# A two-layer model's kernel on one core: the opening of the first block re-ordered, adaLN dots placed anew, row remainders moved from GpSimd to VectorE

## What is computed

```
mod = silu(c) @ ada_w + ada_b                      # 6 x 1024 values; shift1, scale1, gate1, shift2, scale2, gate2
h   = rms_norm(x, norm1_g) * (1 + scale1) + shift1
z   = h @ w_in                                     # 1024 -> 3328: q, k, v of attention, seven parts for RWKV
att = dilated_mixture_attention(norm(q), norm(k), v)   # 8 heads, with a table of biases
rw  = rwkv7_bidirectional(token_shift(z[rest]))
x   = x + gate1 * (concat(att, rw) @ w_out)        # first residual projection
h2  = rms_norm(x, norm2_g) * (1 + scale2) + shift2
x   = x + gate2 * peer_ffn(h2)                     # top-16 experts of 16384, gathered rows
# second block: mod2 = silu(c_2) @ w_ada_2 + b_ada_2, projection 1024 -> 3856, mixers,
# second residual projection, a mixture of 32 experts, final norm
```

## Time and profile before

| | |
|---|---|
| median of three runs | 2759.75 us |
| profiled execution, its own time | 2760.71 us |
| its span, first to last instruction | 2758.7 us |
| TensorE busy in the span | 2326.7 us (84%) |
| VectorE | 1576.8 us (57%) |
| ScalarE | 1024.0 us (37%) |
| GpSimd | 939.3 us (34%) |
| mean granted TensorE clock | 0.950 |
| bytes moved by DMA | 771.20 MB |

### The profile page before, as it was taken

One profiled execution on the slowest core, in us unless ns is written; L12 is line 12 of the kernel. 1 busy time (PEld: TensorE's weight loads), 2 busy tenths in 40 slices (PEclk: granted clock), 3 DMA queues, 4 the chain that ended last, 5 costly groups with the idle time before them and its releaser, 6 DMA issues. The chain is left out here.

```text
span 2758.7 us, 45817 instructions
## 1 busy us (share of the span) xinstructions
PE 2326.7 (84%) x17226; PEld 1389.4 (50%) x17226; DVE 1576.8 (57%) x3636; ACT 1024.0 (37%) x2634; POOL 939.3 (34%) x766
## 2 busy tenths in 40 slices
PE   5998699988999987777777777777789979889996
PEld 4776599956444443322332223322258878643333
DVE  6677756467566667666766667676454363420003
ACT  4436433343233333332333333333254233433333
POOL 0000211131344445555555554555510061223331
PEclk9999899999999999999999999999999956989998
DMA  9624300063999999999999999999922310389994
GB/s 370 229 98 148 133 4 5 5 233 150 383 383 400 381 393 421 421 421 421 414 418 414 411 416 416 414 415 416 414 96 77 108 40 3 128 323 368 367 363 165
DMA packets 156877, 771.20 MB, mean 280 GB/s; under 512 B 34145, under 2 KB 52209, under 8 KB 71153
## 3 DMA queue, kind: packets, MB, share of 16 engines
q0 software_dynamic: 87552, 545.34, 48.7%
q1 hardware_dynamic: 68096, 220.64, 21.2%
q10 hardware_dynamic: 1008, 2.29, 0.2%
HBM read 816.42 MB, written 16.78 MB: 302 GB/s over the span
## 5 line engine op out<-in xcount | busy, mean ns | idle before, releaser
L2182 PE MATMUL bank<-expert_rows,diagonals 128*128 128x512 f32 x1656 | 784.9, 612 | 207.2 <-ACT diagonals L2074 206.4
L1968 POOL DMA_INDIRECT expert_rows<-in_uv,expert_idx x414 | 533.3, 1288 | 580.0 <-PE bank L2182 479.4
L2003 DVE SCALAR_TENSOR_TENSOR expert_rows<-expert_rows,h_rows 128x1024 f32<-128x1024 f32 x414 | 507.6, 1226 | 345.2 <-DMA expert_rows<-in_uv,expert_idx 344.2
L2182 PEld LDWEIGHTS bank<-expert_rows,diagonals 128*128 128x128 f32 x1656 | 303.0, 192 | 637.6 <-ACT diagonals L2074 344.0
L2063 ACT ACTIVATE expert_act<-expert_dot 128x2 f32<-128x2 f32 x256 | 52.0, 203 | 865.9 <-DVE expert_rows L2003 657.0
L2182 PE MATMUL bank<-weight_slots,diagonals 128*128 128x512 f32 x392 | 184.1, 613 | 58.0 <-ACT diagonals L2074 58.0
L2074 ACT ACTIVATE diagonals<-ident,expert_weight 128x128 f32<-128x128 f32 x512 | 173.5, 386 | 0.0
L2003 DVE SCALAR_TENSOR_TENSOR weight_slots<-weight_slots,h_rows 128x1024 f32<-128x1024 f32 x98 | 120.0, 1225 | 88.3 <-DMA weight_slots<-in_uv,expert_idx 84.9
L1968 POOL DMA_INDIRECT weight_slots<-in_uv,expert_idx x98 | 130.1, 1327 | 112.3 <-issue 58.4
L2182 PEld LDWEIGHTS bank<-weight_slots,diagonals 128*128 128x128 f32 x392 | 71.8, 192 | 167.8 <-ACT diagonals L2074 88.6
L761 PE MATMUL bank<-rhs_hi,w_lo 128*128 128x512 f32 (+1 forms) x312 | 128.7, 413 | 28.3 <-DVE w_lo L689 20.4
(11 more groups left out here) (561 smaller groups left out, 4094.0 us busy)
## 6 DMA issues: line engine op xcount, KB each, us to landing
expert_w<-in_experts SPq DMA_DIRECT2D x55, 1024.0 KB, 12.2
expert_w_more<-in_experts SPq DMA_DIRECT2D x41, 1024.0 KB, 10.2
mod_rows<-in_ada_rows SPq DMA_DIRECT2D x34, 1024.0 KB, 7.3
weight_slots<-in_w_in SPq DMA_DIRECT2D x6, 2048.0 KB, 11.2
weight_slots<-in_w_in SPq DMA_DIRECT2D x8, 1536.0 KB, 7.9
mixed<-in_ada_rows SPq DMA_DIRECT2D x8, 1024.0 KB, 4.9
weight_slots<-in_att_bias SPq DMA_DIRECT2D x8, 1024.0 KB
weight_slots<-in_w_out SPq DMA_DIRECT2D x4, 2048.0 KB, 11.1
```

The lines of the kernel that those rows point to most:

```text
L1968: pool.indirect_dma_start(rows[j], None, core.dram["uv"], bass.IndirectOffsetOnAxis(idx[:, t, column:column + 1], 0)).then_inc(arrived[j], 16)
L2003: dve.scalar_tensor_tensor(out=u, in0=u, scalar=1.0, in1=hN[:, t, :], op0=ALU.mult, op1=ALU.mult, accum_out=dot[:, j:j + 1]).then_inc(dott ...
L2182: mm = pe.matmul(bank[2 * (t % 2) + half][:, :], diag[:, j, :], rows[slot_of(n)][:, D + half * S:D + half * S + S], start=column == 0, sto ...
```

## The change

In the first block's opening: x is loaded in two halves ahead of everything; the first two weight items come in halves of four k; shift and scale columns are dotted in pairs of tiles (0 and 4, 1 and 5, ...), so that gain and shift of 256 features are ready after four dots, and the scaling of these two k follows at once; the first two items are multiplied side by side, k by k. The copies of q and k move from one burst per item to chunks 16 to 23. `FIRST` is 28 instead of 24, so 40 filler dots lie in this stage, 8 in attention, 14 in the RWKV inputs, 18 in the first residual projection. In `stage_project` VectorE makes the row remainders in turn with the weight remainders, and scales at most three rows ahead; GpSimd makes none. The second silu moves to chunk 35. The core of the diff:

```diff
-    FIRST, NEEDED, QUARTERS = 24, 16, 96
+    FIRST, NEEDED, QUARTERS = 28, 16, 96
...
-    CHUNKS = [(i, k) for i in range(ITEMS) for k in range(KD)]
+    CHUNKS = [(i, k) for k in range(KD) for i in range(2)] + [(i, k) for i in range(2, ITEMS) for k in range(KD)]
+    FIRST_TWO, HALF = 2 * KD, KD // 2
-    DOTS_AT = [5, 7, 8, 9, 10, 11, 12, 13, 14, 15, 17, 19, 21, 23, 25, 26, 27, 29, 30, 31, 34, 35, 37, 39, 41, 42, 43, 45, 47, 49, 50, 51]
+    DOTS_AT = [17, 18, 19, 21, 22, 23, 24, 25, 25, 26, 27, 29, 29, 30, 31, 32, 33, 34, 34, 35, 37, 38, 39, 41, 43, 45, 46, 46, 47,
+               48, 49, 49, 50, 51, 51, 53, 53, 54, 54, 55]
+    COPY_AT = {16: (0, 1), 17: (2, 3), 18: (4,), 19: (5,), 20: (6,), 21: (7,)}
+    SQUARE_AT = {17: (0, 1), 18: (2,), 19: (3,), 22: (4, 5), 23: (6, 7)}
...
+                for j, part in enumerate((first_half, last_half)):
+                    sp.dma_start(x[:, part, :], xT[:, part, :]).then_inc(x_loaded[j], 16)
                 sp.dma_start(cond, core.dram["c_rows"][0:1, :].rearrange("a n -> (a n)").partition_broadcast(P)).then_inc(c_loaded, 16)
+                sp.dma_start(core.vec[:, :], core.dram["vec"]).then_inc(in_loaded, 16)
...
                 m.load(sp, 0)
+                m.load(sp, 4)
+                weights(first_half, w_first)
                 m.load(sp, 1)
+                m.load(sp, 5)
+                m.load(sp, 2)
+                m.load(sp, 6)
+                weights(last_half, ring.loaded)
+                ring.issued = 2
+                m.load(sp, 3)
+                m.load(sp, 7)
...
-                wanted = [(DOTS_AT[2 * (n - 12) + 1], 0, n) for n in range(12, m.FIRST)] + [(8 * (i - 3) + 7, 1, i) for i in range(3, ITEMS)]
+                wanted = [(DOTS_AT[2 * (n - 12) + 1] - 3, 0, n) for n in range(12, m.FIRST)] + [(8 * (i - 3) + 7, 1, i) for i in range(3, ITEMS)]
...
                 dve.wait_ge(c_squashed, 1)
-                m.dot_some(dve, m.NEEDED)
+                dot_half(0)
+                dot_half(HALF)
                 dve.wait_ge(in_loaded, 64)
-                m.finish(dve, 0, m.NEEDED, [0])
...
+                for j in range(HALF):
+                    gains_of(j)
+                    if j == 0:
+                        dve.wait_ge(inverted, 1)
+                    scale(2 * j)
+                    scale(2 * j + 1)
+                    if 1 <= j < HALF - 1:
+                        dot_half(j + 1)
+                    for k in (2 * j, 2 * j + 1):
+                        row(k)
+                        lower(2 * k)
+                        lower(2 * k + 1)
+                    if j == 0:
+                        dot_half(1)
+                    if j < HALF - 1:
+                        dot_half(HALF + j + 1)
```

`dot_half(n)` is both dots of row tile n; `gains_of(j)` adds the biases to four columns and makes two columns of gain. In `stage_project`, attention and the RWKV inputs:

```diff
+    ROWS = 3
-        LATER_FIRST, LATER_LAST, LATER_AT = 38, 48, range(3, 13)
+        LATER_FIRST, LATER_LAST = 39, 48
+        LATER_AT = [2, 3, 4, 5, 6, 7, 8, 8, 9, 9, 10, 10, 11, 11, 13, 14, 14, 15]
...
+                def row_lower(k):
+                    dve.wait_ge(r_upper, k + 1)
+                    dve.tensor_tensor(r_lo[:, k, :], rhs[:, k, :], r_hi[:, k, :].bitcast(F32), ALU.subtract).then_inc(r_split, 1)
+
-                    if norm is not None and i == 0 and k == 0:
-                        for c in range(CH):
-                            lower(0, c)
-                        for n in range(KD):
+                    if norm is not None and i == 0:
+                        for n in range(0 if k == 0 else k + ROWS - 1, min(k + ROWS, KD)):
...
-                    elif norm is None or i > 0 or k >= CH:
-                        lower(i, k)
+                    if i == 0:
+                        row_lower(k)
+                    lower(i, k)
...
-                for k in range(KD):
-                    pool.wait_ge(r_upper, k + 1)
-                    pool.tensor_tensor(r_lo[:, k, :], rhs[:, k, :], r_hi[:, k, :].bitcast(F32), ALU.subtract).then_inc(r_split, 1)
...
-        DOTS_AT = (3, 5, 8, 10, 13, 15, 18, 20, 23, 25, 28, 30)
+        DOTS_AT = (6, 9, 12, 15, 18, 21, 25, 29)
...
-                    if h < HEADS - 1:
+                    if h < BIASES + 2:
                         m.load(sp, first_half + 2 + h - BIASES)
...
-        FIRST, LAST = 30, 38
+        FIRST, LAST = 32, 39
```

More of the change, by code:

```diff
@@ L480, in _ @@
                 act.activation(rms[:, :], rms[:, :], ACT.Exp, scale=-0.5).then_inc(inverted, 1)
-                row(0)
                 for c, (i, k) in enumerate(CHUNKS):
-                    if k == CH and i >= 1:
+                    if k == CH and i >= 3:
                         evacuate(i - 1)
+                    for j in COPY_AT.get(c, ()):
+                        copy_qk(j)
+                    for j in SQUARE_AT.get(c, ()):
+                        square_qk(j)
+                    if c < FIRST_TWO and i == 0:
+                        row(k)
                     if c in LOG_AT:
@@ L534, in normalise, with dot_half, gains_of @@
                                              op0=ALU.mult, op1=ALU.mult).then_inc(q_normed, 1)
+                two = lambda of, j: of[:, 0:16].rearrange("p (a b) -> p a b", a=2)[:, :, 2 * j:2 * j + 2]
+                def dot_half(n):
+                    m.dot(dve, 2 * n)
+                    m.dot(dve, 2 * n + 1)
+                def gains_of(j):
+                    at = VEC_AT["ada_b"][0]
+                    dve.wait_ge(m.dotted, 4 * (j + 1))
+                    dve.tensor_tensor(two(core.mod, j), two(core.mod, j), two(core.vec[:, at:at + 16], j), ALU.add).then_inc(m.added, 1)
+                    dve.wait_ge(m.added, 2 * j + 1)
+                    dve.scalar_tensor_tensor(out=gain[:, 2 * j:2 * j + 2], in0=core.mod[:, 8 + 2 * j:10 + 2 * j], scalar=1.0,
+                                             in1=core.col("norm1_g", 2 * j, 2), op0=ALU.add, op1=ALU.mult).then_inc(m.added, 1)
+                    dve.wait_ge(m.added, 2 * j + 2)
@@ new lines, in _ @@
+                dve.tensor_tensor(stay[:, :], core.col("mu_prev", 0, 14), core.col("mu_next", 0, 14), ALU.add).then_inc(stay_ready, 1)
+                dve.wait_ge(stay_ready, 1)
+                dve.tensor_scalar(stay[:, :], stay[:, :], -1.0, 1.0, ALU.mult, ALU.add).then_inc(stay_ready, 1)
+                dve.tensor_scalar(gains[:, 0:1], core.col("q_norm_g"), HD ** -0.5, None, ALU.mult).then_inc(gains_ready, 1)
+                dve.tensor_copy(gains[:, 1:2], core.col("k_norm_g")).then_inc(gains_ready, 1)
@@ L545, in _ @@
+                dve.wait_ge(gains_ready, 2)
+                m.next, m.parts_added = m.NEEDED, KD
                 for c, (i, k) in enumerate(CHUNKS):
-                    if k == CH and PLAN[i - 1][0] == "z":
+                    if c < FIRST_TWO:
+                        continue
+                    if k == CH and i >= 3:
                         shift_over(i - 1)
@@ L705, in split @@
                         ahead.on_vector(dve, i * KD + k, r_split, emptied_by)
-                    if later is not None and i * KD + k in LATER_AT:
-                        later.dot_some(dve, 2)
+                    if later is not None:
+                        later.dot_some(dve, LATER_AT.count(i * KD + k))
                 by_chunk(dve, split, lambda f: not on_act(f), dve_emptied)
```

73 lines of the change are left out of this document (32 added, 41 removed).

## The result

Four runs of the changed kernel gave 2735.27, 2739.25, 2741.43 and 2742.78 us, a median of 2740.34; the kernel before gave 2759.44 (2758.26 to 2763.2, four runs). The ratio is 0.9932, interval 0.992 to 0.9945: 19 us (15 to 22) shorter. The forecast was 2737, in a range of 2729 to 2749. The profiled execution was the shortest of the four, 2735.27 us with a span of 2733.5, so its gain of 25.4 us is larger than that of the medians; two more profiles of the same kernel (E0, E11) tell what is the run's own. E1, E4 and E5 stand beside E0, and E8, E9 and E10 beside E11; E2, E3, E6 and E7 have no unedited run beside them.

The account below looks back on a forecast made before the run. TensorE was taken to bind the first projection from first matmul to last, so an earlier start shortens it. Six terms summed to 23.05 us off the profiled 2760.71; as a median, 2737 us, range 2729 to 2749.

Parts of the forecast that it names:

- Opening, 10.7: First projection stage: first matmul at 27.2 instead of 38.89 us, stage ends 10.7 us earlier (bounds 5 and 14.5).
- the low clock at the start: Opening, chunks 0 to 3: 4.2 us at the low clock, as before, costing 2.1 us.
- the gaps of 0.6 and 1.0 us: Opening: TensorE gaps of 0.6 us before chunk 4 and 1 us with hand-over around item 2's weight chunks.
- The 0.5 that I added to the stage's end: Opening's end: the +0.5 in 11.2 - 1.0 + 0.5 = 10.7 us.
- Rival A: Opening gives half because loads or VectorE set its pace: 3 to 6 us there, 13 in all, 2747; chance 0.16.
- Attention, 2.5: Attention: 12 dots become 8 and waits for a tile and a late bias mostly go, 2.5 us (bounds 0.5 and 5).
- rival C: Opening: short VectorE waits keep TensorE at low clock in chunks 4 to 15, 9 us slower, 2769; chance 0.03.
- RWKV inputs, 2.8: RWKV inputs: one row tile less, last two dots and the wait before them go, 2.8 us (bounds 1.5 and 3.2).
- First residual, 4.5: First residual projection: row remainders to VectorE, two dots less, GpSimd silent, 4.5 us (bounds 2.5 and 5.6).
- the budget of 41 against 43.5 us: First residual projection: VectorE needs 41 us against TensorE's 43.5, so TensorE binds.
- Second block 1.9: Second block's projection: three scales instead of eight before the first row, first matmul sooner, 1.9 us (bounds 0.8 and 2.3).
- second residual 0.65: Second residual projection: first matmul 0.65 us earlier (bounds 0 and 1), the rest already at TensorE's pace.

Follow-up runs that it names:

- E0: The changed kernel run again with nothing edited; 2737.86 us, ratio 0.9926 to the kernel before.
- E11: The changed kernel run once more, unedited, beside later runs; 2744.75 us, ratio 0.9956 to the kernel before.
- E1: The changed kernel with two row tiles of attention asked for one place later, behind the biases; 2731.34 us, ratio 0.9912.
- E4: The changed kernel with the table of small vectors (vec) loaded first, ahead of x; 2738.76 us, ratio 0.993.
- E5: The changed kernel with the shared projection stage's eight row-remainder subtractions back on GpSimd; 2740.61 us, ratio 0.9936.
- E8: The changed kernel with both edits, attention's two row tiles asked for later (E1) and vec loaded first (E4); 2732.04 us, ratio 0.9902.
- E9: The changed kernel with attention's first four dots at units 4, 7, 10, 13 instead of 6, 9, 12, 15; 2736.61 us, ratio 0.992.
- E10: The changed kernel with its 18 first-residual dots two to a chunk from chunk 3 to 11; 2743.68 us, ratio 0.9947.
- E2: The kernel before with E7's dot spread plus the change's whole shared stage (row remainders on VectorE, three rows scaled ahead); 2751.94 us, ratio 0.9969.
- E3: The changed kernel with FIRST 24, attention's and the RWKV inputs' dots and loads as before, 20 dots in the residual; 2743.87 us, ratio 0.994.
- E6: The changed kernel with the opening's first two projection items one after the other instead of side by side; 2748.91 us, ratio 0.9963.
- E7: The kernel before with only its 20 first-residual dots spread one or two to a chunk from chunk 2 to 15; 2754.55 us, ratio 0.9983.

## Why the prediction came out

The total was right, and of its six terms four were. Two were not, and gains that I did not have made up for one of them, which is luck. By medians 19 us came of the 23 forecast.

- **Opening, 10.7: right, 10.5**, for the reasons given. The sum of squares began at 11.52 (forecast 11.5, behind vec), the root was there at 23.36 (23.7), the first matmul at 27.12 (27.2), and VectorE's turn for two k held TensorE's pace without a wait. Two small terms partly cancelled: the low clock at the start cost 2.9 us and not 2.1 (0.51 over 6 us), and the gaps of 0.6 and 1.0 us that I had taken off did not come (TensorE idled 0.14 us in the whole projection). The 0.5 that I added to the stage's end has no source in the working. The Trainium skill ("DMA: Bandwidth & Descriptors", Queues, rings and completion order) let a later transfer finish before an earlier one; here vec behind 2.3 MB landed when the order of the queue says, and only when it was asked for first (E4) did the sum begin 3.6 us sooner, which is the size that I gave for it. Rival A's fear, 24 us of VectorE against 21.8 at the end, did not come true, and E6 shows what a pace set by VectorE looks like.
- **Attention, 2.5: wrong.** The gain was nothing in two profiles and a loss of 3.6 in the third, measured from a profile of the kernel before that had a long attention itself: against the same twelve dots in E7, E2 and E3 (77.8 to 78.1) the changed kernel lost 2.3 to 6.1. The step that failed is "the last three bias loads have no row tile ahead of them": true of the last three, but I did not walk the two row tiles left through SyncE's program with the new units. The second tile's load now waits for the dot of unit 15, just when head 5's bias is due, and holds it. E1 shows the term itself: without the blockage the stage falls to 75.2, 5.2 below the first profile and 5.1 below the kernel before, and four dots with their tiles are worth 2.7, which is the 2.5 that I gave. In E0 the rest of the miss is the clock: I had seen in the earlier trace rows that a wait of 2.26 us is followed by a low clock, used that for rival C in the opening, and not here.
- **RWKV inputs, 2.8: right in kind, small.** 4.5 in the first profile, 0.3 and 5.4 in the next two. The ten profiles with fourteen dots average 29.5 us, the four with sixteen 32.7: 3.2. Part of the 4.5 is again the one profile before (33.5; E7 and E2 have 31.1 and 31.6). I gave the two dots and the wait before them; the waits for other row tiles vary by several microseconds from run to run.
- **First residual, 4.5: the size right (3.9 to 5.3, and 0.6 for the first matmul, which is in the column before), the cause wrong.** I gave it to GpSimd falling silent. E5 puts GpSimd back and loses nothing; E7 spreads the dots alone and gains 3.8; E10 bunches them again and loses 3.2 to 4.6. The step that failed is the budget of 41 against 43.5 us for the whole stage: it says that TensorE binds, but not whether two dots at one place outrun four buffers of weights. With GpSimd's subtractions gone they still do, by 2.5 us. That the size came out is luck: the new placement spread the dots as well.
- **Second block 1.9, second residual 0.65: right**, 2.0 and 0.6; of the first, 1.4 is the three rows ahead and not the engine.
- **Not foreseen:** 2.7 to 3.2 us in mixers and experts beyond the second residual's 0.6, partly the clock's timing, and 0.9 to 1.3 in the second block's projection. They stand in for attention's missing 2.5 and for what the unedited profiles fall short elsewhere.

Rival C did not occur. Its mechanism is real on this kernel, in attention above all, but its price was too high: E6 had such waits, and the clock fell for 3.4 us, not for twelve chunks. The Trainium skill ("TensorE: Matmul & The Clock Gate", HAM oscillation) describes bursts with waits between them, each run at the low clock; the windows behind attention's stall (0.61, 0.51) agree, and E6's 0.83 only in part, since its three waits brought one low stretch.

## What to carry to other kernels

When filler work is placed anew, walk every load of it through the issuing queue with its new wait, and look at what is queued behind it and when that is due: here one row tile held a bias back and cost 5 to 9 us, and two changed lines gave them back. A stage's budget doesn't tell whether filler in pairs outruns the buffers; begin with one piece to a chunk, and put pairs later. Where one engine feeds another, widening the work per feed (two items for each row) can be worth more than an earlier start: 9.0 of 10.5 us here.

## What the runs showed of the hardware

The price of a stall of TensorE is not its length. After one and the same stall in attention (6.2 us on VectorE) the mean clock from 215 to 235 us was 0.91 in the first profile and E11 and 0.74 in E0, which is 3.6 and 10.4 us at the lower level, and the stage took 80.4 or 83.9 us; without the stall (E1, E8) the clock stayed at 1.00 there. GpSimd beside VectorE stretches the latter's subtractions (0.68 to a mean of 1.06 us in E5, 1.60 in the kernel before), and yet E5's residual took 53.6 us behind its first matmul, as without it. Ahead of a first matmul, with nothing in store, it cost 0.5 to 0.6 us. That the four weight buffers make this difference is argued, not shown.
